# Linear attention woven into a projection stream: six turns a level instead of four, three turns more before the first level

## The chip, the cores and the metric

The kernel runs on one core of a Trainium2 chip. The metric is device time in microseconds (us) for one execution. Engines are named as in the profile: PE is TensorE (matmul), PEld its weight loads, DVE is VectorE, ACT is ScalarE, POOL is GpSimd, SP issues the transfers.

## The reference, cut to what matters

Two "hybrid" layers over 256 tokens of width 2048, then a second block (a recurrent branch, a gated delta branch and an MLP), all in float32. The part that the change touches is one of the four attention groups of a hybrid layer, gated linear attention with 4 heads:

```python
def gla_chunked(q, k, v, log_a):
    # S_t = diag(a_t) S_{t-1} + k_t^T v_t,  o_t = q_t S_t
    ...
    cum = jnp.cumsum(g_i, axis=2)
    scores = jnp.einsum("bhtd,bhsd,bhtsd->bhts", q_i, k_i, jnp.exp(rel))

def hybrid_layer(x, ...):
    p = split_columns(jnp.einsum("bsd,de->bse", rms_norm(x, norm_g), w_in))
    ...
    gla = from_heads(rms_norm(gla, gla_norm_g)) * jax.nn.silu(p["gla_g"])
    mixed = jnp.concatenate([fox, diff, moba, gla], axis=-1)
    return x + jnp.einsum("bse,ed->bsd", mixed, w_out)
```

The kernel evaluates the decayed scores of all 256 tokens in nine levels of doubling blocks: level `lv` handles the pairs whose positions first differ in bit `lv` (7 down to 0), level -1 the diagonal.

## The kernel before, in words

**Projections.** A layer's input projection is 60 tiles of 128 output columns (`layer_in`), each in two halves of 24 matmuls (three float32r products for each of 8 blocks of rows). A weight half arrives in `wring`, ACT rounds it into a high part (L1329), and DVE (L2048) and POOL (L3023) each subtract one half of it to make the low part; three such `part_L` buffers go round, so ACT can round half h+2 only when PE is through with half h-1. Tiles 0 to 3 are the linear attention's q and k, 4 to 7 its v, 8 to 11 its gate; from tile 12 on come q, k, v, gate of twelve softmax heads (`attend`), one head in four tiles.

**Turns.** Every engine's program is written by the same `Weave`: streams (`layer_in`, `attend`, `gla`, and modulation behind them) are generators, and each `yield` ends a turn; in a turn every stream emits its next piece, `layer_in` first, then `attend`, then `gla`. A tile has four turns, so a turn is 12 projection matmuls on PE. What stands in one turn on one engine runs in order there; engines meet only at semaphores.

**Linear attention (`gla`).** After tile 3 PE computes the decay logits (event `ga`), ACT and DVE turn them into log decays and DVE scans them (L2297). Then for each level: DVE copies the previous level's scores under a mask (`take_scores`, L2305), makes the exponents `gee` (L2319, L2320), ACT takes the exponential `gex` (L1326), DVE multiplies q (`gqe`, L2327), POOL multiplies k (`gke`, L3096), and PE computes the scores `gsc` (8 matmuls of 64x128 at level 7 as the trace counts them, 16 at the others). There is one `ee`, one `qe` and one `ke` buffer and one pair of score banks (ring `GL`), so a level's exponents wait for the previous `gke`, and `gqe`/`gke` wait for the previous `gsc`. After the levels, once tile 11 is said, four heads follow, five turns each: values times scores (`gpv`), squares summed on PE, mean on DVE, root on POOL (`smalls`, L3028), spread on PE.

**Where each piece stands.** Counted in turns from `ga` on, PE's first `gsc` stands at turn 6 and then one every 4 turns; POOL's first `gke` at turn 4 and then every 4. A tile's evacuation is on ACT (copy L1329, tanh L1326) and, for gate tiles, DVE (L2195), in the tile's last turn.

All PE matmuls are issued at L556 (transposes L559).

Of the kernel before, what the change touches and what calls it, by code (L numbers as in the profile page):

```python
# [248 lines left out]
def program(nc, W, WSM, LORA, PARd, CSTd, MSKd, CTX, XIN, XS, ZS, OUT):  # L249
    ctx = ExitStack()  # L250
    with ctx:  # L251
# [293 lines left out]

        LATE_A, LATE_B, LATE_TA, LATE_TB, FIRST_B = 2, 3, 0, 0, 4
        CTXAT = (6, 8, 10, 12)


        def tensor(e):  # L550
# [282 lines left out]
            def gla(l):  # L833
                yield from weave.until(("tile", l, 3))
                (b, _), u = GL.take()
                w.wait_ge(free(GL, u))
                w.wait_ge(done("aT", l))
                for m in range(2):
                    t = mm(b[:, 256 * m:256 * m + 256], P("wa2", 256 * l + 128 * m, 128)[0:16, :], L.aT[0:16, :], True, True)
                t.then_inc(*mark("pe_gla", "ga", l))  # L840
                yield
                yield
                yield
                for lv in range(7, -2, -1):
                    yield
                    yield
                    yield
                    bb, u = GL.take()
                    w.wait_ge(free(GL, u))
                    for t_ in "qk":  # L850
                        for j in range(2):
                            w.wait_ge(done("g" + t_, l, j))
                    if lv >= 0:
                        w.wait_ge(done("gqe", l, lv))
                        w.wait_ge(done("gke", l, lv))
                    qa, ka = (L.qe, L.ke) if lv >= 0 else (L.gq, L.gk)
                    for j in range(4 if lv < 7 else 2):
                        m, hh = (j // 2, j % 2) if lv < 7 else (0, j)
                        ks = slice(128 * m, 128 * m + 128)
                        qs = ks if lv < 7 else slice(128, 256)  # L860
                        for q in range(2):
                            pr = slice(64 * q, 64 * q + 64)
                            t = mm(bb[q][:, 128 * j:128 * j + 128], ka[pr, hh, ks], qa[pr, hh, qs], True, True)
                    t.then_inc(*mark("pe_gla", "gsc", l, lv))
                    yield
                yield from weave.until(("tile", l, 11))
                for h in range(4):
                    (b, b2), u = GL.take()
                    w.wait_ge(free(GL, u))
                    w.wait_ge(done("gst", l, -1))  # L870
                    w.wait_ge(done("gs01", l))
                    w.wait_ge(done("gv", l, h))
                    hs = slice(128 * h, 128 * h + 128)
                    q, hh = h % 2, h // 2
                    mm(b[:, 0:128], L.gv[:, 0, hs], L.ST[:, 4 * q + hh, :], True, True)
                    mm(b[:, 128:256], L.gv[:, 0, hs], L.S01[:, 2 * q + hh, :], True, False)
                    mm(b[:, 128:256], L.gv[:, 1, hs], L.ST[:, 4 * q + 2 + hh, :], False, True).then_inc(*mark("pe_gla", "gpv", l, h))
                    yield
                    yield
                    w.wait_ge(done("sq", ("gla", l, h)))  # L880
                    for m in range(2):
                        t = mm(b2[:, m:m + 1], L.gs[:, 128 * m:128 * m + 128], ones[:, 0:1], True, True)
                    t.then_inc(*mark("pe_gla", "sums", ("gla", l, h)))
                    yield
                    yield
                    w.wait_ge(done("root", ("gla", l, h)))
                    for m in range(2):
                        t = mm(b2[:, 256 + 128 * m:384 + 128 * m], small(3)[:, m:m + 1].broadcast_to([128, 128]), ident, True, True)
                    t.then_inc(*mark("pe_gla", "spread", ("gla", l, h)))
                    yield  # L890
# [429 lines left out]
        def scalar(e):  # L1320
# [197 lines left out]
            def gla(l):  # L1518
                yield from weave.until(("tile", l, 3))
                GL.take()  # L1520
                yield
                w.wait_ge(done("la", l))
                af(L.ee, L.la, ACT.Abs).then_inc(*mark("act_layer"))
                w.wait_ge(last("act_layer"))
                af(L.ee, L.ee, ACT.Exp, scale=-1.0).then_inc(*mark("act_layer"))
                w.wait_ge(last("act_layer"))
                af(L.ee, L.ee, ACT.Ln, bias=1.0).then_inc(*mark("act_layer", "lae", l))
                yield
                yield
                for lv in range(7, -2, -1):  # L1530
                    if lv == 6:
                        w.wait_ge(done("gsc", l, 7))
                        for q in range(2):
                            t = cp(L.S01[:, 2 * q:2 * q + 2, :], bb[q][:, 0:256].rearrange("p (u t) -> p u t", u=2))
                        t.then_inc(*mark("act_layer", "free", "gl", u))
                        counts.at[("gs01", l)] = counts.last("act_layer")
                    if lv >= 0:
                        w.wait_ge(done("gee", l, lv))
                        af(L.ee, L.ee, ACT.Exp).then_inc(*mark("act_layer", "gex", l, lv))
                    yield  # L1540
                    yield
                    yield
                    bb, u = GL.take()
                    yield
                yield from weave.until(("tile", l, 11))
                for h in range(4):
                    (b, b2), u = GL.take()
                    yield
                    w.wait_ge(done("gpv", l, h))
                    w.wait_ge(done("mix", l, 11 + h)) if h else None  # L1550
                    cp(L.go, b[:, 0:256]).then_inc(*mark("act_layer"))
                    w.wait_ge(last("act_layer"))
                    af(L.gs, L.go, ACT.Square).then_inc(*mark("act_layer", "sq", ("gla", l, h)))
                    yield
                    yield
                    yield
                    yield
# [469 lines left out]
        def vector(e):  # L2027
# [252 lines left out]
            def gla(l):  # L2280
# [14 lines left out]
                own(V)  # L2295
                for m in range(2):
                    e.tensor_tensor_scan(L.cum[:, m, :], C("ones", 0, 1).broadcast_to([128, 256]), L.la[:, m, :], 0.0, mult, add).then_inc(*mark(V))  # L2297
                yield

                def take_scores(lv):  # L2300
                    w.wait_ge(done("gsc", l, lv))
# [7 lines left out]
                for lv in range(7, -2, -1):  # L2309
                    if lv < 6:  # L2310
                        take_scores(lv + 1)
                    if lv >= 0:
                        wd = 1 << lv
                        cv = L.cum.rearrange("p m (n two w) -> p (m n) two w", two=2, w=wd)
                        ev = L.ee.rearrange("p m (n two w) -> p (m n) two w", two=2, w=wd)
                        ref = cv[:, :, 0, wd - 1:wd].broadcast_to([128, 256 // wd, wd])
                        own(V)
                        w.wait_ge(done("gke", l, lv + 1)) if lv < 7 else None
                        tt(ev[:, :, 0, :], ref, cv[:, :, 0, :], sub).then_inc(*mark(V))  # L2319
                        tt(ev[:, :, 1, :], cv[:, :, 1, :], ref, sub).then_inc(*mark(V, "gee", l, lv))  # L2320
                    yield
                    if lv >= 0:
                        w.wait_ge(done("gex", l, lv))
                        for j in range(2):
                            w.wait_ge(done("gq", l, j))
                        w.wait_ge(done("gsc", l, lv + 1)) if lv < 7 else None
                        tt(L.qe, L.gq, L.ee, mult).then_inc(*mark(V, "gqe", l, lv))  # L2327
                    yield
                    yield
                    bb, u = GL.take()  # L2330
                    yield
                take_scores(-1)
                yield from weave.until(("tile", l, 11))
                for h in range(4):
                    (b, b2), u = GL.take()
                    yield
# [672 lines left out]
        def gpsimd(e):  # L3009
# [73 lines left out]

            def gla(l):
                yield from weave.until(("tile", l, 3))
                yield
                yield
                yield
                for lv in range(7, -2, -1):
                    yield  # L3090
                    if lv >= 0:
# [2 lines left out]
                            w.wait_ge(done("gk", l, j))  # L3094
                        w.wait_ge(done("gsc", l, lv + 1)) if lv < 7 else None
                        e.tensor_tensor(L.ke, L.gk, L.ee, mult).then_inc(*mark("pool_layer", "gke", l, lv))  # L3096
                    yield
                    yield
                    yield
                yield from weave.until(("tile", l, 11))  # L3100
                for h in range(4):
                    yield
                    yield
# [543 lines left out]
```

## Time and profile before

| | us |
|---|---|
| median of 3 runs | 3913.81 (3911.79 to 3920.32) |
| span of the profiled execution | 3908.8 |
| PE busy | 3701.0 (95%) |
| DVE, ACT, POOL busy | 2097.1, 1503.6, 1661.9 |
| mean granted TensorE clock | 0.977 |
| PE waits for POOL's arena_L L3096, all | 44.4 in 16 |

For the profiled execution only its span (first to last instruction) is given, so that is the time the sum is made against. PE is busy for most of the span, so a stretch in which it is not, or in which its granted clock is below 1.00, is where time can be had.

### The profile page before, as it was taken

The numbers are of one execution on the slowest core, as the hardware profiler recorded it, in microseconds if no ns is written. First come the engines' busy times: TensorE is split into PE (matmuls) and PEld (weight loads), VectorE is DVE, ScalarE is ACT, GpSimd is POOL, SyncE is SP. The second block draws the span as 40 slices with busy tenths as digits, with TensorE's granted clock in tenths as the row PEclk, the third lists the DMA queues.
The fourth block names the chain that finished last, engine by engine and source line by source line (L and its number), as shares of the span: only waits on it lengthen the run. The fifth ranks groups of instructions, "written<-read, shape, count | busy, mean of one in ns | idle before, by whom it ended". The sixth has DMA issues, their size and how long they took to land. (4 is left out here: it accounts for less than half of the span.)

```text
span 3908.8 us, 85968 instructions
## 1 busy us (share of the span) xinstructions
PE 3701.0 (95%) x37216; PEld 3426.5 (88%) x37216; DVE 2097.1 (54%) x3808; ACT 1503.6 (38%) x2641; POOL 1661.9 (43%) x1195
## 2 busy tenths in 40 slices
PE   7899998899998999999979999999998999999998
PEld 6799988799997788888868888888888999999998
DVE  5435434434435776677766666666646553434343
ACT  4344434334444432332223333333334444435343
POOL 4455555455554553333321111111115566666664
PEclk9999998999999999999989999999998999999999
DMA  5355553345444777778610010000006545555553
GB/s 214 128 184 186 192 185 141 140 173 184 162 162 147 251 264 263 246 253 293 222 38 20 24 27 28 19 15 23 6 3 232 178 173 185 182 184 183 184 184 130
DMA packets 116392, 587.21 MB, mean 150 GB/s; under 512 B 20912, under 2 KB 40496, under 8 KB 51376
## 3 DMA queue, kind: packets, MB, share of 16 engines
q1 hardware_dynamic: 116016, 581.71, 41.9%
q8 instruction: 295, 4.83, 0.5%
q14 instruction: 81, 0.66, 0.1%
HBM read 560.95 MB, written 20.71 MB: 149 GB/s over the span
## 5 line engine op out<-in xcount | busy, mean ns | idle before, releaser
L556 PE MATMUL bank<-act_L,part_L 128*128 128x256 f32 x7296 | 958.9, 290 | 10.4 <-DMA cst<-in_cst 4.7
L556 PEld LDWEIGHTS bank<-act_L,part_L 128*128 128x128 f32 x7296 | 913.6, 196 | 48.0 <-issue 28.4
L3023 POOL TENSOR_TENSOR part_L<-wring,part_L 128x512 fp32r<-128x512 f32 x304 | 533.3, 1755 | 550.7 <-ACT part_L L1329 550.7
L556 PE MATMUL bank<-act_P,part_P 128*128 128x512 f32 (+1 forms) x3488 | 716.2, 365 | 17.7 <-POOL part_P L3023 12.9
L3023 POOL TENSOR_TENSOR part_C<-wring,part_C 128x512 fp32r<-128x512 f32 x320 | 569.6, 1789 | 368.9 <-ACT part_C L1329 368.9
L556 PEld LDWEIGHTS bank<-act_P,part_P 128*128 128x128 f32 x3488 | 590.3, 188 | 136.9 <-DVE arena_P L2447 16.1
L556 PE MATMUL bank<-arena_B 64*64 64x64 f32 (+2 forms) x11200 | 542.4, 230 | 38.9 <-DVE arena_B L2560 21.1
L556 PEld LDWEIGHTS bank<-arena_B 64*64 64x64 f32 (+2 forms) x11200 | 479.4, 142 | 88.9 <-DVE arena_B L2560 23.4
L3023 POOL TENSOR_TENSOR part_P<-wring,part_P 128x512 fp32r<-128x512 f32 x184 | 306.0, 1669 | 427.7 <-ACT part_P L1329 427.7
L2048 DVE TENSOR_TENSOR part_L<-wring,part_L 128x512 fp32r<-128x512 f32 x304 | 241.2, 795 | 445.3 <-ACT part_L L1329 445.1
L1329 ACT ACTIVATE part_C<-wring 128x1024 fp32r<-128x1024 f32 x320 | 337.9, 1057 | 360.9 <-PE bank L556 357.9
L556 PE MATMUL bank<-act_Y,part_C 128*128 128x258 f32 (+1 forms) x3840 | 464.6, 283 | 9.4 <-POOL part_C L3023 9.4
L556 PEld LDWEIGHTS bank<-act_Y,part_C 128*128 128x128 f32 x3840 | 463.7, 191 | 9.7 <-issue 9.7
L556 PE MATMUL bank<-act_C,part_C 128*128 128x256 f32 x3840 | 468.5, 283 | 0.0
L556 PEld LDWEIGHTS bank<-act_C,part_C 128*128 128x128 f32 x3840 | 462.6, 192 | 0.0
L1329 ACT ACTIVATE part_L<-wring 128x1024 fp32r<-128x1024 f32 x304 | 319.6, 1054 | 289.2 <-PE bank L556 289.1
L2048 DVE TENSOR_TENSOR part_C<-wring,part_C 128x512 fp32r<-128x512 f32 x320 | 234.1, 731 | 298.5 <-ACT part_C L1329 298.5
L2109 DVE SCALAR_TENSOR_TENSOR arena_P<-arena_P,mods 128x512 f32<-128x512 f32 x240 | 272.8, 1137 | 8.1 <-DMA arena_P<-in_w 4.7
L2048 DVE TENSOR_TENSOR part_P<-wring,part_P 128x512 fp32r<-128x512 f32 x184 | 170.2, 925 | 190.3 <-ACT part_P L1329 190.3
L1329 ACT ACTIVATE part_P<-wring 128x1024 fp32r<-128x1024 f32 x184 | 190.9, 1051 | 153.0 <-PE bank L556 152.4
L3165 POOL COPY arena_B<-cst 128x256 f32<-128x256 f32 x80 | 32.5, 407 | 453.7 <-PE bank L556 453.7
L556 PE MATMUL bank<-wring,arena_B 64*64 64x64 f32 (+3 forms) x2208 | 188.8, 249 | 6.3 <-DVE arena_B L2661 3.1
(250 smaller groups left out, 3430.2 us busy)
## 6 DMA issues: line engine op xcount, KB each, us to landing
wring<-in_w SPq DMA_DIRECT2D x404, 1024.0 KB, 4.8
arena_P<-in_w SPq DMA_DIRECT2D x64, 1024.0 KB, 5.1
mring<-in_w SPq DMA_DIRECT2D x32, 1024.0 KB, 6.4
z_kept<-arena_P SPq DMA_DIRECT2D x34, 256.0 KB, 5.6
z_kept<-arena_P SPq DMA_DIRECT2D x58, 128.0 KB, 5.9
xT<-z_kept SPq DMA_DIRECT2D x26, 256.0 KB, 2.8
arena_C<-z_kept SPq DMA_DIRECT2D x32, 128.0 KB, 3.0
cst<-z_kept SPq DMA_DIRECT2D x24, 128.0 KB, 2.1
```

The source lines that it names most:

```text
L556: return e.matmul(out, lhsT, rhs, start=start, stop=stop)
L1329: return e.activation(out, a, ACT.Copy, scale=scale)
L2048: tt(wl[:, 0:4, :], wring[s % NS][:, 8 * j:8 * j + 4, :], wh[:, 0:4, :].bitcast(F32), sub).then_inc(*mark("dve_lo", "lov", stage, h))
L2109: z = ts(a, x, c, None, mult, None) if row == 0 else stt(a, x, c, a, mult, add)
L3023: e.tensor_tensor(wl[:, 4:8, :], wring[s % NS][:, 8 * j + 4:8 * j + 8, :], wh[:, 4:8, :].bitcast(F32), sub).then_inc(*mark("pool_lo", "lop ...
L3165: e.tensor_copy(region(Q[lv % 2], wd, d), same).then_inc(*mark(sem, "qf", tag, lv))
```

## The change

Two numbers are added: `GLA_LEAD = 3` turns before the first level and `GLA_MORE = 2` turns in each of the nine levels, on all four compute engines alike; and the wait of the heads for tile 11 is taken out, so that the heads follow the levels directly. No instruction is added or removed.

```diff
+        GLA_LEAD, GLA_MORE = 3, 2
...
                 t.then_inc(*mark("pe_gla", "ga", l))
-                yield
-                yield
-                yield
+                yield from weave.rest(3 + GLA_LEAD)
                 for lv in range(7, -2, -1):
-                    yield
-                    yield
-                    yield
+                    yield from weave.rest(3 + GLA_MORE)
                     bb, u = GL.take()
...
                     t.then_inc(*mark("pe_gla", "gsc", l, lv))
                     yield
-                yield from weave.until(("tile", l, 11))
                 for h in range(4):
```

ACT and DVE get the same: the lead before their loops, two turns more between a level's exponential (ACT) or its `gqe` (DVE) and the next level, and no `until`. On POOL:

```diff
                 yield from weave.until(("tile", l, 3))
-                yield
-                yield
-                yield
+                yield from weave.rest(3 + GLA_LEAD)
                 for lv in range(7, -2, -1):
                     yield
...
                         e.tensor_tensor(L.ke, L.gk, L.ee, mult).then_inc(*mark("pool_layer", "gke", l, lv))
-                    yield
-                    yield
-                    yield
-                yield from weave.until(("tile", l, 11))
+                    yield from weave.rest(3 + GLA_MORE)
```

On **PE**, in the first layer, the levels 4, 3 and 2 (`bank<-arena_L 128x128 x8` is one level's scores, `act_L,part_L` are projection products, `mring` a modulation product). Before:

```order
L556 MATMUL bank<-act_L,part_L 128x256 x24
L556 MATMUL bank<-arena_L 128x128 x8
L556 MATMUL bank<-act_L,part_L 128x256 x48
L556 MATMUL bank<-arena_L 128x128 x8
L556 MATMUL bank<-act_L,part_L 128x256 x48
L556 MATMUL bank<-arena_L 128x128 x8
L556 MATMUL bank<-act_L,part_L 128x256 x12
```

And in the changed kernel:

```order
L557 MATMUL bank<-act_L,part_L 128x256 x24
L557 MATMUL bank<-arena_L 128x128 x8
L557 MATMUL bank<-act_L,part_L 128x256 x72
L557 MATMUL bank<-arena_L 128x128 x8
L557 MATMUL bank<-act_L,part_L 128x256 x72
L557 MATMUL bank<-arena_L 128x128 x8
L557 MATMUL bank<-act_L,part_L 128x256 x24
```

Between two levels' scores there are now 72 projection products instead of 48; lines have moved by one.

On **ACT**, where a gate tile and a level meet (`arena_L<-bank` is the tanh of the gate tile, `arena_L<-arena_L` the level's exponential, `part_L<-wring` the rounding of a weight half). Before:

```order
L1326 ACTIVATE arena_L<-bank 128x256 [waits s_pe_proj]
L1326 ACTIVATE arena_L<-arena_L 128x512 [waits s_dve_gla]
L1329 ACTIVATE part_L<-wring 128x1024 [waits s_dma_w1]
L1329 ACTIVATE part_L<-wring 128x1024 [waits s_pe_proj]
L1326 ACTIVATE arena_L<-bank 128x256 [waits s_pe_proj]
L1326 ACTIVATE arena_L<-arena_L 128x512 [waits s_dve_gla]
```

And in the changed kernel:

```order
L1322 ACTIVATE arena_L<-arena_L 128x512 [waits s_dve_gla]
L1322 ACTIVATE arena_L<-bank 128x256 [waits s_pe_proj]
L1325 ACTIVATE part_L<-wring 128x1024 [waits s_dma_w1]
L1325 ACTIVATE part_L<-wring 128x1024 [waits s_pe_proj]
L1322 ACTIVATE arena_L<-bank 128x256 [waits s_pe_proj]
L1325 ACTIVATE part_L<-wring 128x1024 [waits s_dma_w2]
L1322 ACTIVATE arena_L<-arena_L 128x512 [waits s_dve_gla]
```

Before, the exponential stood behind the tanh and in front of the next rounding; now it stands ahead of the tanh or behind a rounding, by turns. On POOL three low parts lie between two `gke` instead of two.

## Rows read from the trace of the kernel before

**Rows 1.** The page: the span and PE's busy time.
```profile
span 3908.8 us, 85968 instructions
...
PE 3701.0 (95%) x37216; PEld 3426.5 (88%) x37216; DVE 2097.1 (54%) x3808; ACT 1503.6 (38%) x2641; POOL 1661.9 (43%) x1195
```

**Rows 2.** Waits of PE, whole span: us in total, times, longest us.
```profile
PE bank L556 <- POOL arena_L L3096: 44.4, 16, 6.6
PE bank L556 <- POOL smalls L3028: 24.2, 25, 2.1
```

**Rows 3.** PE in order of time, first layer: start us, us, instruction [idle before <-releaser].
```profile
65.87 3.17 PE L556 MATMUL bank<-act_L,part_L 128*128 128x256 f32 x24
75.61 1.23 PE L556 MATMUL bank<-arena_L 64*128 64x128 f32 x8 [6.58 <-POOL arena_L L3096]
...
94.53 1.16 PE L556 MATMUL bank<-arena_L 64*128 64x128 f32 x16 [0.20 <-POOL arena_L L3096]
...
103.20 1.16 PE L556 MATMUL bank<-arena_L 64*128 64x128 f32 x16 [1.35 <-POOL arena_L L3096]
104.29 6.02 PE L556 MATMUL bank<-act_L,part_L 128*128 128x256 f32 x48
114.21 1.16 PE L556 MATMUL bank<-arena_L 64*128 64x128 f32 x16 [3.91 <-POOL arena_L L3096]
115.31 7.52 PE L556 MATMUL bank<-act_L,part_L 128*128 128x256 f32 x48
126.36 2.08 PE L556 MATMUL bank<-arena_L 64*128 64x128 f32 x16 [3.54 <-POOL arena_L L3096]
```

**Rows 4.** The same view where the levels of the first layer end.
```profile
160.48 1.16 PE L556 MATMUL bank<-arena_L 64*128 64x128 f32 x16
161.57 1.70 PE L556 MATMUL bank<-act_L,part_L 128*128 128x256 f32 x12
163.11 0.93 PE L556 MATMUL bank<-arena_L 128*128 128x128 f32 x6
```

**Rows 5.** The same view of the second layer: before the first level, and the last.
```profile
656.50 3.11 PE L556 MATMUL bank<-act_L,part_L 128*128 128x256 f32 x24
665.97 1.23 PE L556 MATMUL bank<-arena_L 64*128 64x128 f32 x8 [6.36 <-POOL arena_L L3096]
...
750.82 1.16 PE L556 MATMUL bank<-arena_L 64*128 64x128 f32 x16
```

**Rows 6.** Stretches: us, busy of PE, PEld, DVE, ACT, POOL, granted clock, DMA share, GB/s.
```profile
69.00:160.50 91.50, 69.03 (x529) 63.77 (x528) 50.94 (x61) 27.48 (x40) 43.11 (x26) 0.85 0.34 125
...
300.00:350.00 50.00, 50.00 (x414) 48.25 (x414) 26.01 (x55) 23.36 (x45) 27.97 (x21) 1.00 0.52 190
```

**Rows 7.** DVE in order of time: one level's work behind a gate tile.
```profile
106.44 0.42 DVE L2195 SCALAR_TENSOR_TENSOR arena_L<-arena_L,bank 128x256 f32<-128x256 f32 x1 [2.85 <-ACT arena_L L1326]
106.78 1.36 DVE L2305 COPY_PREDICATED arena_L<-msk,bank 128x512 f32<-128x512 uint8 x2
108.18 0.43 DVE L2319 TENSOR_TENSOR arena_L<-arena_L 128x256 f32<-128x256 f32 x1
```

**Rows 8.** ACT in order of time: the same level.
```profile
106.03 0.38 ACT L1326 ACTIVATE arena_L<-bank 128x256 f32<-128x256 f32 x1 [4.52 <-PE bank L556]
108.97 0.63 ACT L1326 ACTIVATE arena_L<-arena_L 128x512 f32<-128x512 f32 x1 [2.56 <-DVE arena_L L2320]
109.51 1.99 ACT L1329 ACTIVATE part_L<-wring 128x1024 fp32r<-128x1024 f32 x2
```

**Rows 9.** POOL in order of time: the same level.
```profile
110.63 1.77 POOL L3023 TENSOR_TENSOR part_L<-wring,part_L 128x512 fp32r<-128x512 f32 x1 [5.89 <-ACT part_L L1329]
112.36 1.71 POOL L3096 TENSOR_TENSOR arena_L<-arena_L 128x512 f32<-128x512 f32 x1
```

**Rows 10.** DVE in order of time: exponents beside a busy POOL; low parts with POOL and without.
```profile
74.27 1.75 DVE L2048 TENSOR_TENSOR part_L<-wring,part_L 128x512 fp32r<-128x512 f32 x1
75.94 1.49 DVE L2319 TENSOR_TENSOR arena_L<-arena_L 128x256 f32<-128x256 f32 x1
...
82.16 0.69 DVE L2048 TENSOR_TENSOR part_L<-wring,part_L 128x512 fp32r<-128x512 f32 x1 [4.41 <-ACT part_L L1329]
```

**Rows 11.** DVE in order of time: the last level's mask copy.
```profile
161.69 1.36 DVE L2305 COPY_PREDICATED arena_L<-msk,bank 128x512 f32<-128x512 uint8 x2 [0.76 <-PE bank L556]
```

More of the change, by code:

```diff
@@ L1527, in gla @@
                 af(L.ee, L.ee, ACT.Ln, bias=1.0).then_inc(*mark("act_layer", "lae", l))
-                yield
-                yield
+                yield from weave.rest(2 + GLA_LEAD)
                 for lv in range(7, -2, -1):
@@ L2297, in gla @@
                     e.tensor_tensor_scan(L.cum[:, m, :], C("ones", 0, 1).broadcast_to([128, 256]), L.la[:, m, :], 0.0, mult, add).then_inc(*mark(V))
-                yield
+                yield from weave.rest(1 + GLA_LEAD)
                 def take_scores(lv):
@@ L2327, in gla @@
                         tt(L.qe, L.gq, L.ee, mult).then_inc(*mark(V, "gqe", l, lv))
-                    yield
-                    yield
+                    yield from weave.rest(2 + GLA_MORE)
                     bb, u = GL.take()
@@ L2332, in gla @@
                 take_scores(-1)
-                yield from weave.until(("tile", l, 11))
                 for h in range(4):
@@ L3085, in gla @@
                 yield from weave.until(("tile", l, 3))
-                yield
-                yield
-                yield
+                yield from weave.rest(3 + GLA_LEAD)
                 for lv in range(7, -2, -1):
@@ L3096, in gla @@
                         e.tensor_tensor(L.ke, L.gk, L.ee, mult).then_inc(*mark("pool_layer", "gke", l, lv))
[L3097 to L3100, printed above, removed]
+                    yield from weave.rest(3 + GLA_MORE)
                 for h in range(4):
```

## The prediction

> **What bounds the kernel now.** I read the page first: PE is busy for 95% of the span of 3908.8 us [rows 1], so a change can only pay where PE stands still or runs slowly. The waits of PE come next. The largest is for POOL's arena_L at L3096, the multiplied keys `gke` of a level: 44.4 us in 16 waits, eight in each layer, one for every level from 7 to 0 [rows 2]. The timeline says what such a wait is made of. Level 7 comes 6.58 us after its turn, the levels that meet no gate tile wait 0.20 and 1.35 us, those that meet one wait 3.91 and 3.54 us [rows 3]. Last, the stretches: from the first wait to the last level the granted clock is 0.85, while in a stretch where PE has no pause it is 1.00 [rows 6]. After the wait of 3.91 us the same 48 products that took 6.02 us take 7.52 us, and the next scores 2.08 instead of 1.16 us: PE is at 1.2 GHz instead of 2.4 there. So the levels cost twice, by the pause and by what it does to the clock.
>
> **What the stretch costs beyond its work.** In layer one it runs from 65.87 + 3.17 = 69.04 to 160.48 us, 91.44 us [rows 3, 4]; in layer two from 656.50 + 3.11 = 659.61 to 750.82, 91.21 us [rows 5]. Its work at full clock: 8 times 48 products at 6.02 us, 48.2; seven score groups that move the next start by 104.29 - 103.20 = 1.09 us, 7.6; level 7's half-size group, 0.6 (half of it); four transposes and two modulation products, 2.6 by their starts in the same timeline. Together 59.0 us. What is left is 32.4 + 32.2 = 64.6 us for the two layers. Of it 44.4 are waits [rows 2] and 20.2 the low clock.
>
> **The chain of one level, and what the change does to it.** Behind a gate tile it goes, from scores to scores, 103.20 to 114.21, 11.01 us: PE does 12 more products to the tile's end; ACT's tanh starts at 106.03; DVE's gating follows at 106.44, and only behind it the mask copy at 106.78 (1.36 us) and the exponents at 108.18 [rows 7]; the exponential at 108.97 (0.63), then the rounding of a weight half, 1.99 us for two [rows 8]; POOL's low part of the first at 110.63 (1.77), and `gke` behind it at 112.36 (1.71) [rows 9]. PE's own work in between is 1.09 + 6.02 = 7.1 us, which leaves the 3.9 us of wait. Without a gate tile the chain is 103.20 - 94.53 = 8.67 us [rows 3], against the same 7.1 and the tile's transposes.
>
> *Two more turns a level.* A level is now followed by 72 products: 1.5 x 6.02 = 9.0, with the scores 10.1 us of work. Even if the chain stayed as it is, 8.67 us would fit, and behind a gate tile 11.0 - 10.1 = 0.9 us would be left, at 4 or fewer levels a layer, 7 us in all. The chain also gets shorter. Six turns are a tile and a half, so a level now starts at a tile's end or in its middle by turns. At a tile's end the gating stands beside the scores, not 12 products later; in the middle the exponential stands ahead of the tanh; and in both the rounding and the low part come before the exponential instead of between it and `gke`. What is left is the scores (1.16), DVE's start some 0.8 us later (0.76 in [rows 11]), copy 1.36, exponents 0.8, exponential 0.6, `gke` 1.7 and the hand-overs, some 0.2 each: about 7 us against 10.1. I take the level waits as zero and keep 0 and 7 us as ends.
>
> *Three more turns of lead.* With the first level's own two they put level 7 five turns later, 5 x 1.5 = 7.5 us, against a wait of 6.58 us [rows 3]. `gke` itself may move by up to three turns, but its place on POOL is now four turns ahead of the scores instead of two (6 us for 1.71 us of work). Zero left.
>
> *The clock.* With no pause the levels should run as the later heads do, at 1.00 [rows 6]. The 20.2 us come back.
>
> *The heads directly behind the levels.* The levels now end 5 + 8 x 2 = 21 turns later, behind tile 18, so the `until` for tile 11 would be met anyway: removing it costs and gives nothing. The last level's scores now stand at a tile's end. `gpv` comes one turn (12 products, 1.5 us) behind them and needs the mask copy. Before, the copy started at 161.69 and ended just as PE came to `gpv` at 163.11 [rows 4, 11]. Now a rounding (about 1.0) and a low part (0.69) [rows 8, 10] that can only begin at the tile's end are ahead of it: 0.2 + 1.0 + 0.2 + 0.7 = 2.1, plus 1.4 for the copy is 3.5 us, against 1.1 + 1.5 = 2.6 us of PE's work. That is a new wait of about 0.9 us a layer, 2 us if the low part goes at its slow 1.75 us [rows 10]. I take 1.3 a layer, 2.6 together; the ends are 0 and 4.2. The heads' waits for roots (`smalls`) stay: five turns a head go through the four places in a tile, before as now, only in another order.
>
> *What may come late next.* POOL's low part behind `gke`. Counted from a tile's end with scores, `gke` ends after about 7 us (8.1 with the overlap of the next paragraph) and the low part 1.8 later, at 8.8 to 9.9; PE wants that half after three halves (3 x 3.0) and two score groups (2 x 1.1), at 11.2 us. No wait, with 1.3 us to spare.
>
> **One price that decides little, by row and by page.** DVE's exponents took 1.49 us instead of 0.43 when POOL was at work, and a low part 1.75 instead of 0.69 [rows 7, 10]. In the new order POOL's low part runs while DVE copies the mask, so the exponents may meet its end: up to 1.1 us a level, against some 3 us to spare. *The Trainium skill ("SBUF — State Buffer", section on the two separate sides) says that VectorE and GpSimd share a port pair as an exclusive lock: a VectorE instruction with two SBUF inputs and a GpSimd instruction that reads SBUF stop each other for their whole length. By it the exponents begin behind POOL's low part or wait for all of it, and a level that meets the lock twice loses over 2 us of its slack; that speaks for the second case below.* The sum goes by the rows: no wait.
>
> **The sum.** -44.4 - 20.2 + 2.6 = -62.0 us. Against the profiled span: 3908.8 - 62.0 = 3846.8. The median stands 5.0 us above that span, so the forecast for the median is 3913.8 - 62.0 = **3852**. The profiled execution's span and the runs agree well enough that I carry the difference over whole.
>
> **The rivals.**
> 1. *Waits shrink but do not go.* Slack is lost to the DVE/POOL overlap and, from tile 15 on, to the softmax heads' work on DVE. The gate levels keep 7 us and the eight heads wait for their roots 2.1 us each, the longest seen [rows 2], 17 instead of 3 us. Time 3852 + 7 + 14 = 3873. For it: levels 1, 0 and -1 and all heads now lie beside softmax heads. Against: in the earlier place the last two of four linear heads did too. Chance 0.12.
> 2. *The pauses go, the clock stays low* for a reason that isn't the pauses: 3852 + 20 = 3872. Against it: 0.85 is seen here and 1.00 right behind [rows 6]. Chance 0.04.
> 3. *The wait travels with the turns.* Each engine holds a level's pieces until its own turn; if the positions and not the time set the wait, moving all four alike changes nothing, and the time stays at 3914. Against: `gke` was four turns behind the last scores and two ahead of its own, and is now two and four; positions did not move alike. Chance 0.04.
> 4. *Slower: weights come late.* Each level's `gke` (1.71) and the low part queued behind it (1.77) [rows 9] would hold back the next half's weights at every level, since three `part_L` buffers allow no more run ahead. That puts a wait of 3.5 us at PE's first product of that half at 16 levels, 56 us, and the clock's 20 us again: 3852 + 76 = 3928. It decides from the point where the low part lands more than 1.3 us later than counted above; to be slower than before it must do so by all 3.5 us at nearly every level. Against: POOL is busy for 43 of 91 us there [rows 6]. Chance 0.03.
>
> **How the numbers follow.** My forecast has 0.77, the rivals 0.12, 0.04, 0.04 and 0.03. Its own ends: with no new wait at the heads, and the heads' and other small waits of the stretch (some 4 us) gone too, 3852 - 3 - 4 = 3845, and 3 us for the measurement, 3842; with 7 us of level waits left, 3859. To hold 8 in 10 with sizes uncertain the range has to reach to rivals 1 and 2: 3842 to 3876. A difference of about 0.2% (8 us) is what a measurement of this kernel can tell from none. Faster by more than that are my case and rivals 1 and 2: 0.93. Rival 3 is the same, 0.04, rival 4 slower, 0.03.
>
> **What would show it.** In the profile after: PE's waits for POOL's arena_L fall from 44.4 us to under 7; the granted clock between the first and the last level is 1.00 in both layers; one period from scores to scores is about 10.1 us at every level; a wait of about 1 us for DVE's arena_L stands before the first head's `gpv`. The forecast is wrong if PE waits for part_L (rival 4), if periods stay at 11 us with a clock under 1.00, or if `smalls` waits grow by more than 5 us.

## The result, and the profile after

The changed kernel takes **3849.7 us** (median; 3848.5 to 3852.9) against 3912.8 us for the one before on the same chip: a ratio of 0.984 with a 95% interval of 0.983 to 0.985. The forecast was 3852 us with a range of 3842 to 3876. The profiled span fell from 3908.8 to 3846.6 us, by 62.2; the forecast sum was 62.0. How far its terms were right is another matter, and the experiments below show that the change holds two remedies for one wait, of which one alone brings all of the gain and the other alone most of it.

The page after the change, span and busy times (answers to [rows 1]):

```profile
span 3846.6 us, 85962 instructions
...
PE 3682.1 (96%) x37216; PEld 3409.0 (89%) x37216; DVE 2084.0 (54%) x3808; ACT 1504.8 (39%) x2641; POOL 1659.3 (43%) x1195
```

PE has the same 37216 matmuls; it is busy 18.9 us less, which is matmuls no longer run at the low clock. Source lines have moved by more than one on the other engines: ACT's L1326 and L1329 are now L1322 and L1325; DVE's low part L2048, mask copy L2305, exponents L2319 and L2320 and `gqe` L2327 are L2040, L2297, L2311, L2312 and L2319; POOL's low part L3023, roots L3028 and `gke` L3096 are L3013, L3018 and L3084. The waits of PE, whole span (to [rows 2]; us in total, times, longest):

```profile
PE bank L557 <- POOL smalls L3018: 22.2, 22, 2.1
...
PE bank L557 <- issue: 3.2, 2, 1.7
...
PE bank L560 <- ACT arena_L L1325: 1.0, 2, 0.5
...
PE bank L557 <- DVE arena_L L2297: 0.9, 2, 0.5
```

There is no row for POOL's arena_L any more: the 44.4 us in 16 waits are gone. Three small rows are new (the last three shown), 5.1 us together. PE in order of time in the first layer (to [rows 3]):

```profile
98.62 1.16 PE L557 MATMUL bank<-arena_L 64*128 64x128 f32 x16
99.71 6.02 PE L557 MATMUL bank<-act_L,part_L 128*128 128x256 f32 x48
...
109.72 1.16 PE L557 MATMUL bank<-arena_L 64*128 64x128 f32 x16
110.81 8.90 PE L557 MATMUL bank<-act_L,part_L 128*128 128x256 f32 x72
119.64 1.16 PE L557 MATMUL bank<-arena_L 64*128 64x128 f32 x16
```

From scores to scores it is 9.92 us (109.72 to 119.64), all of it work, and 48 products take 6.02 us. And the stretches (to [rows 6]), from the first to the last level's scores of layer one (the small new waits lie ahead of it), and the same later stretch:

```profile
77.80:164.40 86.60, 86.55 (x754) 81.43 (x753) 49.12 (x74) 35.86 (x54) 54.23 (x32) 1.00 0.50 183
300.00:350.00 50.00, 50.00 (x414) 48.09 (x411) 23.54 (x49) 23.83 (x46) 27.96 (x20) 1.00 0.52 189
```

PE is busy for 86.55 of 86.60 us and the granted clock is 1.00, where it was 0.85. In layer two, from 638 to 724 us, it is 1.00 as well.

**One level behind a gate tile, after.** DVE, ACT and POOL in order of time (to [rows 7, 8, 9]); the scores before it began at 109.72:

```profile
110.91 0.69 DVE L2040 TENSOR_TENSOR part_L<-wring,part_L 128x512 fp32r<-128x512 f32 x1 [3.09 <-ACT part_L L1325]
111.52 1.36 DVE L2297 COPY_PREDICATED arena_L<-msk,bank 128x512 f32<-128x512 uint8 x2
112.91 0.43 DVE L2311 TENSOR_TENSOR arena_L<-arena_L 128x256 f32<-128x256 f32 x1
113.25 0.42 DVE L2312 TENSOR_TENSOR arena_L<-arena_L 128x256 f32<-128x256 f32 x1
114.64 0.42 DVE L2187 SCALAR_TENSOR_TENSOR arena_L<-arena_L,bank 128x256 f32<-128x256 f32 x1 [0.97 <-ACT arena_L L1322]
114.98 1.28 DVE L2319 TENSOR_TENSOR arena_L<-arena_L 128x512 f32<-128x512 f32 x1
```
```profile
109.82 1.06 ACT L1325 ACTIVATE part_L<-wring 128x1024 fp32r<-128x1024 f32 x1 [2.73 <-PE bank L557]
113.71 0.63 ACT L1322 ACTIVATE arena_L<-arena_L 128x512 f32<-128x512 f32 x1 [2.83 <-DVE arena_L L2312]
114.25 0.37 ACT L1322 ACTIVATE arena_L<-bank 128x256 f32<-128x256 f32 x1
```
```profile
110.96 1.81 POOL L3013 TENSOR_TENSOR part_L<-wring,part_L 128x512 fp32r<-128x512 f32 x1 [1.99 <-PE bank L557]
114.42 1.30 POOL L3084 TENSOR_TENSOR arena_L<-arena_L 128x512 f32<-128x512 f32 x1 [1.65 <-ACT arena_L L1322]
```

The rounding (109.82) and the low parts (110.91, 110.96) now lie ahead of the exponential (113.71), and the tanh (114.25) behind it. The chain ends with `gqe` at 116.26: 6.5 us after the scores began, where it had been 11.0. At the other place that the levels come to, a tile's end, `gke` is done at 105.40, 6.8 us after the scores at 98.62. Either would even fit into the 7.1 us of work of the old four turns, which raised the question that the experiments answer.

### The profile page after: what moved, and what is told of

Read it like the earlier page. It is cut to its first block and busy times, and to the rows that moved or that the text cites. A ratio compares the mean times of both kernels' runs of the same rounds, so it can differ in the third digit from the quotient of the medians.

```text
span 3846.6 us, 85962 instructions
## 1 busy us (share of the span) xinstructions
PE 3682.1 (96%) x37216; PEld 3409.0 (89%) x37216; DVE 2084.0 (54%) x3808; ACT 1504.8 (39%) x2641; POOL 1659.3 (43%) x1195
## 5 line engine op out<-in xcount | busy, mean ns | idle before, releaser
L557 PE MATMUL bank<-act_L,part_L 128*128 128x256 f32 x7296 | 946.6, 288 | 12.4 <-DMA cst<-in_cst 4.6
L557 PEld LDWEIGHTS bank<-act_L,part_L 128*128 128x128 f32 x7296 | 901.0, 193 | 49.1 <-issue 30.6
L3013 POOL TENSOR_TENSOR part_L<-wring,part_L 128x512 fp32r<-128x512 f32 x304 | 532.8, 1754 | 458.0 <-ACT part_L L1325 449.7
L3013 POOL TENSOR_TENSOR part_C<-wring,part_C 128x512 fp32r<-128x512 f32 x320 | 567.6, 1782 | 370.1 <-ACT part_C L1325 370.1
L3013 POOL TENSOR_TENSOR part_P<-wring,part_P 128x512 fp32r<-128x512 f32 x184 | 306.1, 1669 | 428.1 <-ACT part_P L1325 428.1
L1325 ACT ACTIVATE part_C<-wring 128x1024 fp32r<-128x1024 f32 x320 | 338.4, 1058 | 355.8 <-PE bank L557 352.7
L2040 DVE TENSOR_TENSOR part_L<-wring,part_L 128x512 fp32r<-128x512 f32 x304 | 239.5, 789 | 426.0 <-ACT part_L L1325 425.8
L1325 ACT ACTIVATE part_L<-wring 128x1024 fp32r<-128x1024 f32 x304 | 320.6, 1056 | 293.5 <-PE bank L557 293.5
L2040 DVE TENSOR_TENSOR part_C<-wring,part_C 128x512 fp32r<-128x512 f32 x320 | 235.7, 736 | 297.9 <-ACT part_C L1325 297.8
L2040 DVE TENSOR_TENSOR part_P<-wring,part_P 128x512 fp32r<-128x512 f32 x184 | 170.2, 925 | 190.9 <-ACT part_P L1325 190.8
L1325 ACT ACTIVATE part_P<-wring 128x1024 fp32r<-128x1024 f32 x184 | 191.2, 1053 | 153.0 <-PE bank L557 152.4
L1325 ACT ACTIVATE arena_B<-bank 128x128 f32<-128x128 f32 (+4 forms) x296 | 111.2, 394 | 216.9 <-PE bank L557 119.3
```

The source lines that it names most:

```text
L557: return e.matmul(out, lhsT, rhs, start=start, stop=stop)
L1325: return e.activation(out, a, ACT.Copy, scale=scale)
L2040: tt(wl[:, 0:4, :], wring[s % NS][:, 8 * j:8 * j + 4, :], wh[:, 0:4, :].bitcast(F32), sub).then_inc(*mark("dve_lo", "lov", stage, h))
L3013: e.tensor_tensor(wl[:, 4:8, :], wring[s % NS][:, 8 * j + 4:8 * j + 8, :], wh[:, 4:8, :].bitcast(F32), sub).then_inc(*mark("pool_lo", "lop ...
```

## Experiments

Each kernel is the changed one with the edit shown, unless it says otherwise; times are medians, each with the kernel before on the same chip.

### Two turns more without the lead

```diff
-        GLA_LEAD, GLA_MORE = 3, 2
+        GLA_LEAD, GLA_MORE = 0, 2
```

> The change with its lead of three turns taken back (GLA_LEAD 0, GLA_MORE 2). If a level waits because too little of PE's work lies ahead of it, level 7 now comes 2 turns (3.0 us) later than in the kernel before, where it waited 6.6 us: a wait of about 3.6 us for gke in each layer and some 2.6 us of low clock behind it, no or small (under 1 us) waits at the other levels: about 3850 + 12 = 3862 us, less up to 3 us because the pause covers the short wait for low parts that the changed kernel has behind the decay logits. Rival, that the lead does nothing: 3850 us.

Measured: 3855.2 us against 3910.6, ratio 0.986 (0.985 to 0.988). Most of the gain is there without the lead. The lead is worth 5 to 9 us (by the medians, and by the ratios to the kernel before), where 12 were expected, and the wait stands in another place than expected:

```profile
72.97 2.77 PE L557 MATMUL bank<-act_L,part_L 128*128 128x256 f32 x12 [3.47 <-POOL part_L L3013]
75.55 0.63 PE L560 MATMUL bank<-cst,arena_L 128*128 128x128 f32 x2
76.11 0.90 PE L557 MATMUL bank<-arena_L 64*128 64x128 f32 x8
```

That is PE in order of time. It waits 3.47 us for a low part of the weights, not for `gke`, and the scores of level 7 right behind (76.11) wait for nothing. The low part is POOL's at 71.05 (1.77 us), which stands ahead of the first `gke` (72.79) and not behind it, so this is not the mechanism of the prediction's fourth rival. It was late because ACT's rounding for it (69.94) stands behind the exponential of level 7 (69.40), which waited 3.46 us for DVE's exponents; with the lead the roundings go ahead of that exponential. In layer two the wait is 3.26 us. Twelve products behind it take 2.77 us instead of 1.7: the clock fell here too, to a granted clock of 0.66 between 73 and 78 us.

The two turns more do not work by their length alone. A level every six turns stands in the old place, the middle of a tile's second half, only every other time, and with the end of a gate tile behind it only once a layer. There the chain is as long as before: from the scores at 107.20 `gke` is done at 118.13, 10.9 us later. In layer one a modulation product fills the rest; in layer two PE waits 0.81 us at 679.70, for the low part that stands ahead of that `gke`; the prediction had 0.9 us for such a level. Without the end of a gate tile, 10.1 us of work cover the 8.7 us of the chain.

### The lead without more turns a level

```diff
-        GLA_LEAD, GLA_MORE = 3, 2
+        GLA_LEAD, GLA_MORE = 3, 0
```

> The change with its two more turns a level taken back (GLA_LEAD 3, GLA_MORE 0). Two theories differ widely. Spacing: four turns (7.1 us of work) are too few for a chain of 8.7 to 11.0 us, the waits of levels 6 to 0 (16 us a layer) and most of their low clock stay: about 3912.8 - 18 = 3895 us. Place: three turns of lead put every level at the end of a tile's first half, where the exponential stands ahead of the gate tile's tanh and behind the rounding; in the changed kernel's trace the chain at that place is 109.72 to 116.26, 6.6 us to the end of gqe, under 7.1 us: hardly any wait, 3846 to 3858 us. I hold place for the likelier, 0.6.

Measured: 3846.6 us against 3910.6, ratio 0.984 (0.982 to 0.985). With four turns a level, as before the change, no wait for `gke` is left in the list of PE's waits. PE in order of time:

```profile
96.44 1.16 PE L557 MATMUL bank<-arena_L 64*128 64x128 f32 x16
97.53 6.02 PE L557 MATMUL bank<-act_L,part_L 128*128 128x256 f32 x48
103.48 1.16 PE L557 MATMUL bank<-arena_L 64*128 64x128 f32 x16
```

From scores to scores it is 7.04 us, pure work, while in the kernel before the same four turns took 11.0 us beside gate tiles. What differs is where in a tile the level stands: three turns later in a cycle of four, which is the end of the tile's first half instead of the middle of its second. Which link of the new order counts most is read from the traces only; no run moved one alone. The same level on DVE and POOL:

```profile
101.70 1.28 DVE L2319 TENSOR_TENSOR arena_L<-arena_L 128x512 f32<-128x512 f32 x1
```
```profile
101.13 1.30 POOL L3084 TENSOR_TENSOR arena_L<-arena_L 128x512 f32<-128x512 f32 x1 [1.66 <-ACT arena_L L1322]
102.39 1.73 POOL L3013 TENSOR_TENSOR part_L<-wring,part_L 128x512 fp32r<-128x512 f32 x1
```

`gqe` ends at 102.98, half a microsecond before the scores at 103.48 need it.

### A lead of four, and of five

```diff
-        GLA_LEAD, GLA_MORE = 3, 2
+        GLA_LEAD, GLA_MORE = 4, 0
```

> Four turns a level as in the kernel before, and a lead of four turns instead of three: one turn (1.5 us of PE's work) more room ahead of the first level than the lead-only kernel, which measured 3846.6 us. The only other difference is that every level falls back into the middle of a tile's second half, where it stood in the kernel before. Place theory: the long chains return, 3.9 us of wait at the four levels beside gate tiles, about 1.3 us at the other three, some 18 us a layer, and 7.5 us of low clock with them: 3846.6 + 51 = about 3897 us. Lead theory (the time ahead of the first level is what counted): 3847 us or less.

Measured: **3898.1 us** against 3912.6, ratio 0.996 (0.994 to 0.997). One turn more of lead costs some 50 us, since every level is back in the middle of a second half. PE's waits and PE in order of time:

```profile
PE bank L557 <- POOL arena_L L3084: 36.0, 16, 3.9
```
```profile
95.36 6.02 PE L557 MATMUL bank<-act_L,part_L 128*128 128x256 f32 x48
105.28 1.21 PE L557 MATMUL bank<-arena_L 64*128 64x128 f32 x16 [3.90 <-POOL arena_L L3084]
106.42 7.43 PE L557 MATMUL bank<-act_L,part_L 128*128 128x256 f32 x48
117.57 2.08 PE L557 MATMUL bank<-arena_L 64*128 64x128 f32 x16 [3.72 <-POOL arena_L L3084]
```

The 3.9 us, the 7.43 for 48 products and the scores at 2.08 are those of [rows 3]. With `GLA_LEAD, GLA_MORE = 5, 0` every level stands at a tile's end:

> Four turns a level and a lead of five: the scores of every level stand at a tile's end, a third place. With a lead of three (end of the first half) the kernel took 3846.6 us, with four (middle of the second half) 3898.1 us. Place theory, by the changed kernel's trace at a tile's end: scores at 98.62, gke done at 105.40, 6.8 us against 7.1 us of PE's work, so no waits for gke above 0.3 us and a time of 3846 to 3851 us. If the time merely grows with the lead beyond three turns, it is above 3890 us.

Measured: 3849.2 us against 3908.7, ratio 0.984 (0.983 to 0.986), with no wait for `gke`. So the time does not follow the lead; only one of these three places is bad. The fourth, the middle of a tile's first half, was not tried with four turns a level.

### Five turns a level

```diff
-        GLA_LEAD, GLA_MORE = 3, 2
+        GLA_LEAD, GLA_MORE = 3, 1
```

> The changed kernel with five turns a level (GLA_LEAD 3, GLA_MORE 1). Five turns walk through all four places of a tile; only the level whose scores stand in the middle of gate tile 11's second half has the long chain (11.0 us against 8.6 us of work). Place theory: one wait of about 2.4 us a layer with up to 1.5 us of clock: 3849.7 + 5 to 8 = 3853 to 3857 us. If only the number of turns a level counted, five would lie half way between four turns in the old place and six: about 3875 us, with a wait at most levels.

Measured: 3853.6 us against 3912.6, ratio 0.985 (0.983 to 0.987). PE in order of time between 70 and 160 us, the two rows that wait for `gke`:

```profile
102.79 1.16 PE L557 MATMUL bank<-arena_L 64*128 64x128 f32 x16 [0.17 <-POOL arena_L L3084]
...
123.47 1.16 PE L557 MATMUL bank<-arena_L 64*128 64x128 f32 x16 [2.48 <-POOL arena_L L3084]
```

The one long wait is 2.48 us, against 2.4 worked out, and it stands behind the one level that falls into the middle of a gate tile's second half. In layer two the same level waits 1.32 us, since a modulation product of 1.0 us stands in between; from scores to scores it is 11.0 us in both layers (112.44 to 123.47, 675.52 to 686.56). The row of 0.17 us follows a level in the middle of a first half: 94.07 to 102.79, a chain of 8.7 us, which the 7.1 us of four turns would not cover.

### The clock by itself

The kernel before, with matmuls into the still unused score bank; all outputs are computed as before.

```diff
                     w.wait_ge(free(GL, u))
+                    for f in range({7: 48, 3: 24, 2: 24, 1: 24, 0: 24}.get(lv, 0)):
+                        mm(bb[0][:, 0:256], L.act[:, f % 16, 0, 0:128], L.act[:, f % 16, 0, :], True, True)
                     for t_ in "qk":
```

> The kernel before, with projection-sized matmuls into the level's still unused score bank ahead of the scores: 48 at level 7, 24 at each of the levels 3 to 0, so that PE works through most of a pause. The output is unchanged, since the scores overwrite the bank. It prices the clock alone. If the clock falls because of the pauses and costs 20 us, the time falls by about 20 us though no chain is shorter: 3893 us, with waits for gke of 0.6 us at level 7 and about 0.9 us at levels 3 to 0, and a granted clock of 1.00 between the levels. If the low clock costs nothing or is not due to the pauses: 3913 us or more.

Measured: 3895.8 us against 3910.6, ratio 0.996 (0.995 to 0.998); the profiled spans are 3890.4 against 3908.8. 288 matmuls more make the kernel 15 us (18 by the spans) faster. PE in order of time, and the stretch:

```profile
102.06 6.02 PE L556 MATMUL bank<-act_L,part_L 128*128 128x256 f32 x48
107.92 3.04 PE L556 MATMUL bank<-act_L 128*128 128x256 f32 x24
112.01 1.16 PE L556 MATMUL bank<-arena_L 64*128 64x128 f32 x16 [1.05 <-POOL arena_L L3098]
113.11 6.02 PE L556 MATMUL bank<-act_L,part_L 128*128 128x256 f32 x48
```
```profile
69.00:160.00 91.00, 83.83 (x737) 79.28 (x737) 53.41 (x65) 30.35 (x45) 46.84 (x28) 1.00 0.38 137
```

The chain behind a gate tile is still 11.0 us (100.97 to 112.01), but the granted clock is 1.00. So the low clock came from the pauses and cost 15 to 18 us of its own (the ratio's interval allows 9 to 20); 20.2 had been worked out.

### POOL's `gke` two turns later, and three times over

```diff
                 for lv in range(7, -2, -1):
-                    yield
+                    yield from weave.rest(1 + 2)
                     if lv >= 0:
...
-                    yield from weave.rest(3 + GLA_MORE)
+                    yield from weave.rest(3 + GLA_MORE - 2)
```

> The changed kernel with POOL's gke two turns later in every level (two turns ahead of the scores, as in the kernel before, instead of four), levels still six turns apart. By the count of the chain, gke would end 9.1 to 9.6 us after the last scores began, against 10.1 us of PE's work: no wait above 0.5 us, 3850 to 3856 us. If it was gke's own place ahead of the scores that removed the waits, they come back at the levels beside gate tiles: 3 us at four levels a layer and the clock with them, about 3850 + 24 + 12 = 3886 us.

Measured: 3851.3 us against 3910.6, ratio 0.985 (0.983 to 0.986), and no wait for `gke`. That `gke` now stands four turns ahead of the scores instead of two is worth nothing. The second edit takes up POOL's time there:

```diff
+                        for _ in range(2):
+                            e.tensor_tensor(L.ke, L.gk, L.ee, mult).then_inc(*mark("pool_layer"))
+                            w.wait_ge(last("pool_layer"))
                         e.tensor_tensor(L.ke, L.gk, L.ee, mult).then_inc(*mark("pool_layer", "gke", l, lv))
```

> The changed kernel with gke computed three times over at each level on POOL (same result), 3.4 to 3.6 us more of POOL's time in a place where I counted 3 us to spare for the scores and 1.3 us for the low part of the weights queued behind it. If the count holds, PE waits for gke by about 0.5 us a level and for low parts of the weights (part_L) by 1.2 to 2.3 us at each of 16 levels: 3850 + 20 to 40 = about 3878 us. If POOL has no such tight place, the time stays within 5 us of 3850.

Measured: 3858.9 us against 3912.6, ratio 0.986 (0.985 to 0.988). 9 us, not 28. PE's waits, and POOL in order of time at one level:

```profile
PE bank L557 <- POOL arena_L L3087: 3.7, 7, 1.0
...
PE bank L557 <- POOL part_L L3013: 2.4, 5, 0.5
```
```profile
104.66 3.50 POOL L3085 TENSOR_TENSOR arena_L<-arena_L 128x512 f32<-128x512 f32 x2 [1.36 <-ACT arena_L L1322]
108.24 1.62 POOL L3087 TENSOR_TENSOR arena_L<-arena_L 128x512 f32<-128x512 f32 x1
109.82 4.24 POOL L3013 TENSOR_TENSOR part_L<-wring,part_L 128x512 fp32r<-128x512 f32 x3
```

The second and third pass add 3.4 us to the 1.8 of one, and the three low parts behind take 1.4 us each (4.24 in all), faster than the 1.77 of [rows 9]. The places that I had called tight are there (both rows of waits are new). For `gke` the count holds about, 0.5 us a wait, though at 7 levels of 16; for the low part it was 0.7 to 1.8 us too tight: PE waits for one 0.5 us at the most, not 1.2 to 2.3. The fourth rival was further off than the 1.3 us from which the prediction let it begin.

### The new small wait, and a better version

The changed kernel has a wait that the prediction had not foreseen, 1.70 us named "issue", with 0.50 us for ACT behind it, in each layer. PE, DVE and POOL there, in order of time:

```profile
70.97 1.66 PE L557 MATMUL bank<-act_L,part_L 128*128 128x256 f32 x12 [1.70 <-issue]
73.13 0.44 PE L560 MATMUL bank<-cst,arena_L 128*128 128x128 f32 x2 [0.50 <-ACT arena_L L1325]
```
```profile
64.78 1.79 DVE L2112 SCALAR_TENSOR_TENSOR arena_L<-arena_L 128x512 f32<-128x512 f32 x1
66.60 1.41 DVE L2026 TENSOR_SCALAR arena_L<-arena_L 128x512 f32<-128x512 f32 x1
68.05 2.24 DVE L2289 TENSOR_TENSOR_SCAN arena_L<-cst,arena_L 128x256 f32<-128x256 f32 x2
70.21 1.26 DVE L2040 TENSOR_TENSOR part_L<-wring,part_L 128x512 fp32r<-128x512 f32 x2
```
```profile
64.22 4.94 POOL L3013 TENSOR_TENSOR part_L<-wring,part_L 128x512 fp32r<-128x512 f32 x3 [4.90 <-ACT part_L L1325]
```

"issue" says that the profile names no releaser. PE goes on at 70.97, as soon as DVE's first low part (70.21, half of 1.26 us) is there. DVE's log decays and scan stand ahead of it in one turn, and POOL's three low parts, whose roundings follow ACT's own functions closely (63.09, 64.31, 66.36), run beside them. That makes the block slower too: from 64.78 to 70.21 it takes 5.4 us, where the same four instructions took 3.5 us in the kernel before (66.00 to 69.54), with POOL idle from 67.2 on. The edit moves ACT's Ln and DVE's block one turn on, and the memset behind the logits, in the lead-only kernel:

```diff
                 af(L.ee, L.ee, ACT.Exp, scale=-1.0).then_inc(*mark("act_layer"))
+                yield
                 w.wait_ge(last("act_layer"))
                 af(L.ee, L.ee, ACT.Ln, bias=1.0).then_inc(*mark("act_layer", "lae", l))
...
-                e.memset(L.ST, 0.0).then_inc(*mark(V))
                 yield
                 w.wait_ge(done("ga", l))
...
                 counts.at[("la", l)] = counts.last(V)
+                e.memset(L.ST, 0.0).then_inc(*mark(V))
+                yield
                 yield
                 logsig(L.la, L.ee, V, ("lae", l), "ls", l)
```

(One turn is taken off the lead on both engines in return.)

> The lead-only kernel (GLA_LEAD 3, GLA_MORE 0, 3846.6 us) with the log decays spread out: ACT's Ln and DVE's log, scale and scan one turn later, and DVE's memset of the score sums behind the decay logits instead of ahead of them. If the 1.7 us that PE waits at the third tile half after the logits in each layer, and the 0.5 us for ACT behind it, come from that block holding up ACT's roundings and DVE's low parts, both go: -4.4 us, about 3842 us. If they come from something else, the time stays at 3846 to 3847 us and the waits stay where they are.

Measured: 3846.9 us (3839.4 to 3848.4) against 3912.6, ratio 0.983 (0.981 to 0.984). The row "issue" is gone from PE's waits, the wait for ACT is 0.7 instead of 0.5 us; but the time was that of the lead-only kernel, with runs so far apart that 3 us could not be told. The three kernels again, on one chip:

> The changed kernel again, beside the two below on the same chip: 3849 us; by the waits that the traces show, 3 us above the lead-only kernel, since two turns more a level bring nothing but a place later in the layer.

> The lead-only kernel again: 3846 us; if the two more turns a level are worth anything, it is slower than the changed kernel here.

> The lead-only kernel with spread log decays again: its trace lacks 3.2 us of waits for low parts but its first timing did not show them. If they are real and nothing takes their place: 3 us below the lead-only kernel, 3843 us; if they are given back elsewhere, the same time as the lead-only kernel.

| kernel | median us | runs | ratio to before |
|---|---|---|---|
| the change (lead 3, six turns) | 3850.3 | 3846.8 to 3852.5 | 0.985 (0.983 to 0.986) |
| lead 3, four turns | 3846.8 | 3845.2 to 3851.2 | 0.984 (0.983 to 0.985) |
| the same, log decays spread | **3843.1** | 3842.8 to 3844.3 | 0.983 (0.982 to 0.984) |

All runs of the third lie below all runs of the other two, 7.2 us below the change by the medians. The intervals of the three ratios overlap, and the first four runs of the same kernel (3839.4 to 3848.4) did not lie below the lead-only kernel; that each step is worth 3 to 4 us rests on the medians here and on the waits in the traces, and is likely rather than shown. The wait of 3.2 us in all is shown gone, and its cause, the block of work for the decays ahead of the low parts, is shown by moving it; which of the three moved pieces did it was not tried one by one.

## Why the prediction was right

*The stretch and what it cost beyond its work.* Right. It put 64.6 us there, 44.4 of waits and 20.2 of clock. In the trace after, nothing waits for `gke` and the clock is 1.00. The clock's term was mis-sized by a little, if at all: PE is busy 18.9 us less after the change, and the kernel with filled pauses gave 15 us by the medians and 18 by the spans.

*Two more turns a level.* The chain was placed rightly: about 7 us at both places that the levels come to, 6.5 and 6.8 measured. One of its terms was misread: the 0.76 us of [rows 11] are DVE's idle time ahead of the mask copy, not a delay behind the scores (the scores ended at 161.64, the copy began at 161.69); after the change DVE's low part of 0.69 us stands there (110.91), which the sum did not count, so the two about cancel. And the step counted as the remedy what is one of two. The text gave the 72 products the first place and "The chain also gets shorter" the second. Four turns in a good place take 3846.6 us, the same four in the old place 3898.1; the shorter chain alone does all of it, and the room is needed only where a level stands in a bad place (five turns: 2.48 and 1.32 us, once a layer). The sum could not tell, since both remedies together leave nothing to wait for.

*Three turns of lead.* Priced as the end of the 6.58 us wait ahead of level 7. It does that, but more important, it shifts the levels by three places in a cycle of four, which the prediction did not price by itself. By the medians the lead alone is worth 64 us, the turns alone 55, both together 63.

*The heads directly behind the levels.* The new wait ahead of `gpv` is there, 0.47 us in each layer for DVE's mask copy (0.9 together); 2.6 had been taken, with 0 and 4.2 as ends. DVE's side was counted rightly (the copy ends at 167.84, 3.4 us after the scores at 164.41, against 3.5), and its low part took its fast 0.69 us. PE's side was not: two transposes stand there (167.04), so it had 3.0 us of work instead of 2.6. The waits for roots stayed, 22.2 instead of 24.2 us.

*What may come late next.* Here a step failed, though by little. It looked for late low parts behind `gke` and found none, as in the trace. It did not look ahead of the first level, where DVE and ACT work on the log decays: 3.2 + 1.0 us of new waits. The old wait of 6.58 us most likely covered them. The errors cancelled: +0.9 for the heads, +4.2 here, -2.0 for roots and -1.2 in a wait ahead of the layers (for DVE's arena_L L2378, 12.4 us instead of 13.6, which moves between 11.6 and 13.3 in these runs with no part of the change), together +1.9 where 2.6 had been put. With the 64.6 that makes 62.7, against the measured 62.2. That the sum came within 0.2 us is luck.

*The rivals.* "Waits shrink but do not go" and "the clock stays low" are refuted by the trace after, "the wait travels with the turns" by the time. That last one held a true half, which its text missed: the positions do set the wait, only not all alike. The argument against it also misstated them: before, `gke` stood two turns behind the last scores, not four, and two ahead of its own; now it is two and four. "Weights come late" was seen in small when `gke` was made three times as long (2.4 us in all). The late low parts of the kernel without the lead (3.47 and 3.26 us) had another cause, the exponential ahead of ACT's rounding.

*The rule on the shared port pair.* Behind the gate tile the exponents did not meet POOL's low part (0.43 and 0.42 us in the rows above); at level 6 they did, as the Trainium skill ("SBUF — State Buffer", section on the two separate sides) would have it (POOL's low part ran there from 79.32 to 81.12):

```profile
79.89 1.52 DVE L2311 TENSOR_TENSOR arena_L<-arena_L 128x256 f32<-128x256 f32 x1
```

The 1.1 us lost there stayed within the slack, and no wait of PE followed.

## What to carry to other kernels

Where engines are kept in step by a common cycle of turns, a level of a dependent chain has a place in the cycle as well as a distance to the next, and what stands ahead of each link in each in-order queue depends on the place: try every offset of the cycle before buying distance. Here the right offset gave the whole gain, and two turns more on top of it gave nothing (3850.3 against 3846.8 us). When a change holds two remedies, a right sum says nothing about which one works; take each away alone. And a large wait that is removed may have covered a small one ahead of it: look at what each engine does just ahead of the old wait, not only behind it.

## What the runs showed of the hardware that was not expected

- More work made the kernel faster: 288 filler matmuls in the pauses took 15 us off, because PE stayed at 2.4 GHz (granted clock 1.00) instead of falling to 1.2 GHz after pauses of 3.5 to 3.9 us; 48 products behind such a pause took 6.02 us instead of 7.52. In the kernel with five turns one pause of 2.48 us was enough: the 60 products behind it took 8.95 us instead of 7.46.
- DVE instructions with a single tensor as input also become slower beside POOL: the scaling of 128x512 took 1.41 us with POOL at work and 0.43 in the spread kernel with POOL idle (65.39; POOL idle from 64.56 to 65.92). Of those with two inputs, the scan of the log decays (two of 128x256) took 2.24 us beside POOL and 1.27 without. The mask copy, which reads its scores from a PSUM bank, did not become slower: 1.36 us at 111.52, with POOL's low part running from 110.96 to 112.77.
- Which of DVE and POOL starts first decided which one was slow. In the changed kernel a `gke` at 103.60, just behind DVE's `gqe` (103.55, 0.69 us), took 1.80 us; one at 114.42, ahead of `gqe` (114.98), took 1.30, and then `gqe` took 1.28.
